# The last norm of a two-layer step: three tiles by ScalarE and GpSimd, two by VectorE

## The reference, cut to what matters

```
x = x + gate2 * hierarchical_moe(h2, ...)
...
def rms_norm(x, g):
    xf = x.astype(jnp.float32)
    y = xf * lax.rsqrt(jnp.mean(xf * xf, axis=-1, keepdims=True) + EPS)
    return (y * g.astype(jnp.float32)).astype(x.dtype)

y_prompt = rms_norm(xp, final_norm)
y_sample = rms_norm(xs, final_norm)
```

## Time and profile before

| | us |
|---|---|
| median of 3 runs | 1088.19 |
| lowest and highest of them | 1087.49, 1089.31 |
| the profiled execution: its time | 1088.57 |
| the profiled execution: its span | 1086.6 |

### The profile page before, as it was taken

One profiled execution on the slowest core, in us unless ns is written; L12 is line 12 of the kernel. 1 busy time (PEld: TensorE's weight loads), 2 busy tenths in 40 slices (PEclk: granted clock), 3 DMA queues, 4 the chain that ended last, 5 costly groups with the idle time before them and its releaser, 6 DMA issues.

```text
span 1086.6 us, 16043 instructions
## 1 busy us (share of the span) xinstructions
PE 993.7 (91%) x5720; PEld 765.0 (70%) x5720; DVE 672.6 (62%) x966; ACT 585.9 (54%) x929; POOL 250.6 (23%) x304
## 2 busy tenths in 40 slices
PE   5999989997998799999989999899779969999994
PEld 2688865765776588877847888467668758888771
DVE  0359125655256799889653941465635679998956
ACT  4452235655233488888366321465633348898822
POOL 3033016211041122231310410620112321222031
PEclk9999998998899899999999999899999989999997
DMA  9785226643155999999780240556423269999954
GB/s 317 268 274 199 78 63 252 225 157 117 59 209 196 345 388 411 404 403 359 257 267 19 83 150 10 198 184 228 154 97 136 85 231 344 411 420 407 370 188 173
DMA packets 89091, 248.17 MB, mean 228 GB/s; under 512 B 25772, under 2 KB 30380, under 8 KB 79816
## 3 DMA queue, kind: packets, MB, share of 16 engines
q1 hardware_dynamic: 75960, 209.54, 51.9%
q0 software_dynamic: 11632, 32.60, 8.5%
q10 hardware_dynamic: 1440, 5.24, 1.2%
HBM read 220.82 MB, written 30.21 MB: 231 GB/s over the span
## 4 chain that ended last, share of the span: by engine, by line
PE 66%; DMA 11%; DVE 9%; ACT 7%; issue 4%; SPq 1%; POOL 0%; ACTq 0%; POOLq 0%; DVEq 0%
PE ps L1592 11%; PE ps L1594 11%; PE ps L1593 11%; DMA pool<-in_moe_w 6%; PE ps L1610 4%; DMA raw<-in_moe_w 3%; PE ps L1788 3%; PE ps L1803 3%; PE ps L1599 3%; PE ps L1601 3%; PE ps L1600 3%; DVE wL L1378 2%; PE ps L1777 2%; ACT wH L960 2%; PE ps L2027 2%
## 5 line engine op out<-in xcount | busy, mean ns | idle before, releaser
L1592 PE MATMUL ps<-wH,actH 128*128 128x512 f32 x600 | 243.0, 405 | 6.1 <-DVE actL L1127 2.5
L1594 PE MATMUL ps<-wH,actL 128*128 128x512 f32 x600 | 235.8, 393 | 0.0
L1593 PE MATMUL ps<-wL,actH 128*128 128x512 f32 x600 | 235.0, 392 | 0.0
L1378 DVE TENSOR_TENSOR wL<-raw,wH 128x2048 fp32r<-128x2048 f32 x64 | 146.3, 2287 | 13.0 <-ACT wH L960 12.7
L1592 PEld LDWEIGHTS ps<-wH,actH 128*128 128x128 f32 x600 | 113.7, 189 | 33.9 <-issue 6.2
L960 ACT ACTIVATE wH<-raw 128x2048 fp32r<-128x2048 f32 x64 | 122.3, 1913 | 25.6 <-DMA raw<-in_moe_w 25.6
L1594 PEld LDWEIGHTS ps<-wH,actL 128*128 128x128 f32 x600 | 113.3, 189 | 25.1
L1593 PEld LDWEIGHTS ps<-wL,actH 128*128 128x128 f32 x600 | 113.8, 190 | 21.5
L1599 PE MATMUL ps<-wH,actH 128*128 128x512 f32 x256 | 104.1, 407 | 6.1 <-DVE actL L1499 3.4
L1601 PE MATMUL ps<-wH,actL 128*128 128x512 f32 x256 | 100.8, 394 | 0.0
L1600 PE MATMUL ps<-wL,actH 128*128 128x512 f32 x256 | 99.8, 390 | 0.0
(11 more groups left out here) (270 smaller groups left out, 1715.3 us busy)
## 6 DMA issues: line engine op xcount, KB each, us to landing
raw<-in_moe_w SPq DMA_DIRECT2D x96, 512.0 KB, 8.3
raw<-in_w_ada SPq DMA_DIRECT2D x40, 1024.0 KB, 5.0
raw<-in_moe_w SPq DMA_DIRECT2D x16, 1024.0 KB, 13.9
pool<-in_moe_w SPq DMA_DIRECT2D x32, 512.0 KB, 7.9
pool<-in_moe_w SPq DMA_DIRECT2D x16, 1024.0 KB, 13.1
ys<-pool SPq DMA_DIRECT2D x32, 512.0 KB, 12.9
raw<-in_w_in SPq DMA_DIRECT2D x15, 1024.0 KB, 8.9
raw<-in_w_ada SPq DMA_DIRECT2D x16, 512.0 KB, 12.2
```

Of the source, the lines that this page charges most:

```text
L1378: dve.tensor_tensor(wL[:, w, :], mraw[parity][i], f32(wH[:, w, :]), ALU.subtract).then_inc(sem(f"m_lo{i}"), 1)
L1592: pe.matmul(out, aH, wH[:, slot_, cols_], start=first, stop=False)
L1593: pe.matmul(out, aH, wL[:, slot_, cols_], start=False, stop=False)
L1594: return pe.matmul(out, aL, wH[:, slot_, cols_], start=False, stop=last)
```

## The change

For tiles 0, 1 and 2 the final norm leaves VectorE. ScalarE does the product with the factor per token (`norm1_scale` into `xr[t]`, the form that layers 0 and 1 begin with), and GpSimd then multiplies by `frow` (`final_row`, a new function) and writes `x[:, t, :]`. Tiles 3 and 4 stay with `final_norm` on VectorE; ahead of the first of these VectorE waits until the three products of GpSimd are done, so that `y_final` counts the tiles in order. GpSimd's product for tile t-1 stands behind its `rstd` pair of tile t, and ScalarE's scaling of tile t-1 behind its squaring of tile t.

```
+TAIL = 3
...
-                rstd1(l + 1)
+                if l + 1 < DEPTH:
+                    rstd1(l + 1)
+            l = DEPTH
+
+            def final_row(t):
+                pl.wait_ge(sem("xr_ready"), at("xr_ready", l, t + 1))
+                pl.tensor_tensor(x[:, t, :], xr[t], frow, ALU.mult).then_inc(sem("y_final"), 1)
+
+            pl.wait_ge(sem("final_row"), 16)
+            for t in range(NT):
+                rstd(stat[:, t:t + 1], stat[:, 8 + t:9 + t], 1, D, sem("ss1"), at("ss1", l, t + 1), sem("rstd1"))
+                if 1 <= t <= TAIL:
+                    final_row(t - 1)
...
             def norm1_scale(l, t):
 
-                if l < DEPTH:
+                if l < DEPTH or t < TAIL:
...
             def final_norm(t):
+                if t == TAIL:
+                    dve.wait_ge(sem("y_final"), TAIL)
...
-                    if l == DEPTH - 1 and t:
+                    if l == DEPTH - 1 and t > TAIL:
                         final_norm(t - 1)
```

## The result

The changed kernel takes 1091.01 us (median of 7 runs, 1089.11 to 1095.08), the kernel before on the same chip 1087.93 (7 runs, 1085.23 to 1090.86). The ratio is 1.0030, with a 95% interval of 1.0016 to 1.0044: slower by some 3.3 us, between 1.7 and 4.8. The interval holds the forecast of +3.2 and also the +4.4 of the prediction's first rival; the trace tells them apart, not the time.

A forecast was written before the change was run, and what follows sets the result against it. GpSimd's last rstd pair, with its 9.5 us drain, was taken to bound the kernel; products and adds holding each other delay it from 1076.92 to 1080.11, +3.2 on the median 1088.19: 1091.4 us, range 1089.6 to 1093.4.

The forecast's parts named there:

- the prediction's first rival: At tile 2, GpSimd's first product wins over VectorE's add and TensorE ends late: +4.4, 1092.6 us; chance 0.28.
- first product, held: GpSimd's product for tile 0 asks 0.09 behind the add of tile 2, is held, and ends at 1069.73.
- end of the last pair: GpSimd's rstd pair of tile 4, behind the third product: ends at 1080.11, 3.2 us later than before.
- The bound: At the kernel's end, GpSimd's last rstd pair sets the time, with its 9.5 us closing drain behind it.
- The rival of the untied drain: GpSimd's closing drain isn't tied to its last instruction and still ends at 1086.4: +-0, 1088.2 us; chance 0.09.
- The price of a product: Each of GpSimd's new 128x1024 products costs 2.36 us, with bounds of 2.32 and 2.56.
- The exclusion: VectorE's two-SBUF-input and GpSimd's SBUF-reading instructions exclude each other: end 3.2 us later with it, 0.4 earlier without.
- One order inside the tail: First half of tile 4's pair beside the norm of tile 3, second half held by it until 1080.11.
- The sign of an add of tile 4 over 2 us long: Expected in the new trace: VectorE's add of tile 4 (L1587), held by GpSimd's second product, over 2 us long.
- The rival without exclusion: GpSimd's products and VectorE's adds run side by side, adds at TensorE's pace: -0.4, 1087.8 us; chance 0.08.
- The rival of the first product: GpSimd's first product goes ahead of tile 2's add, delaying TensorE's tile 4: +4.4, 1092.6 us; chance 0.28.

The follow-up runs named there:

- the pairs taken away: Kernel before, factors per token of tiles 3 and 4 (or tile 4 alone) made by ScalarE and VectorE, not GpSimd: 0.9955 (tile 4 alone: 0.9970) against before.
- the run with memsets: Changed kernel with each of GpSimd's three products replaced by a memset of the same length that reads no SBUF: 0.9989 against the kernel before.
- The run with the late add: Changed kernel with a 256-column memset on VectorE ahead of tile 2's product, so tile 2's add comes after GpSimd's first product begins: 1.0047 against before.
- the run through PSUM: Changed kernel with VectorE's gate-row product written back to PSUM in the last tail, so the add has one SBUF input: 1.0021 against the kernel before.

## Why the prediction was right

Each time below counts from TensorE's last matmul (1071.90 in the prediction's sum, 1069.15 in the trace after); the predicted ones are those of the sum.

| step | predicted | measured |
|---|---|---|
| first product, held | 3.36 long | 3.29 |
| second and third product | 2.36 long | 2.35, 2.34 |
| end of the add of tile 4 | 3.27 | 3.17 |
| end of the last pair | 8.21 | 8.16 |
| end of the last norm | 9.59 | 9.55 |
| end of the span | 17.9 | 17.9 |

- **The bound** (GpSimd's last pair, with the drain behind it) held, and was open when the prediction was made: one drain in one trace couldn't show what it hangs on. The extra memset on GpSimd, the extra norms on VectorE and the pairs taken away show it from three sides. The rival of the untied drain falls.
- **The price of a product**, from the line through 512 and 1280 columns, was right to 0.02 us. The estimate of 2.25 from the Trainium skill ("GPSIMD Engine Reference", Performance versus the Vector engine) was 0.1 too low, and the trace's rows decided rightly.
- **The exclusion** was the term that carried the sum, and its offset of 0.14 (the held instruction needs its own length less that) fits: the add of tile 4 ends at 1072.32, which is the product's end at 1071.24 + 1.23 - 0.15. The rule of the Trainium skill ("SBUF — State Buffer", Who interferes with whom) agrees with the traces, also in that a GpSimd instruction which only writes doesn't conflict with VectorE's two inputs (memsets of 2.40 beside adds of 1.22). That the holder keeps the other out for its whole length stands there of VectorE's two-port modes; for two-input instructions the product of 3.29 and the add of 3.20 show it here.
- **One order inside the tail was wrong.** The prediction let the first half of the last pair in ahead of the norm of tile 3, and had its second half held. In the trace the norm goes first (1075.35, against 1075.39), the first half takes 1.28 and the second is free (0.55, where about 1 was named as a sign). From the end of the third product to the end of the pair it is 2.00 and not 1.82. That the total came out at 8.16 against 8.21 is luck by these 0.2 us: the third product had ended 0.23 earlier than summed (6.16 against 6.39). The sign of an add of tile 4 over 2 us long wasn't met either: it took 1.87, and the prediction's own sum gave 1.98.
- **The rival without exclusion falls**, since the add of tile 4 took 1.87 and not 1.23 beside a product. Its price of -0.4 was for a chip in which nothing is held, and no run is that case: with memsets and through PSUM the last pair ends 0.7 to 0.8 above before, because the norm of tile 3 still holds half of it. Without these 1.1 us the run with memsets would have ended its pair at 5.77 - 1.09 = 4.68, which is 0.3 under the 5.02 of before, so the price fits. What a reader can take from the two runs is that even with the adds free the tail ends 0.7 to 0.8 later than before.
- **The rival of the first product** was not what the trace shows, by a margin of 0.16 (1063.58 against 1063.74; predicted 0.09). The run with the late add shows that it costs 1.4 more, where 1.2 was worked out. The order can turn by itself: in the trace of the run through PSUM TensorE waited 0.78 for a gather ahead of tile 2, and the product came first (1064.93 against 1064.99). Whether some of the seven runs of the changed kernel fell into it isn't known: their times spread by 6 us, those of before by 5.6, and only one has a trace.

## What to carry to other kernels

Before work is moved from VectorE to GpSimd, look at what both do at that moment: a two-input elementwise instruction on each, all in SBUF, is not parallel work but a queue of two, and a chain that goes from one to the other pays in both directions. In these traces an input in PSUM took VectorE out of the conflict. Then look past the last computing instruction at each queue's closing drain: in this kernel GpSimd's took 9.5 us in all nine traces, so two pairs of 0.8 us taken from GpSimd's end gave 5.5 us of tail, while 2.5 us more on VectorE cost at most 0.2. Whether a kernel without gathers on GpSimd has the same drain wasn't tried.

## What the runs showed of the hardware that was not expected

- GpSimd's closing drain lasts 9.5 us from the end of its last instruction: 10.08 from its start in seven of the eight traces with the pair last (10.09 in the other), and 13.09 with a memset of 3.08 behind the pair. ScalarE's and VectorE's end with their last instruction (in the kernel before at 1076.0 and 1078.4, with the last instructions ending at 1076.0 and 1078.3). What the 9.5 us are spent on no run shows.
- VectorE writing a product back to PSUM and adding from there costs nothing: both instructions keep 1.22 to 1.23 us for 128x1024.
- A delay of 0.3 us turns an order and moves the end by 1.4: with the add of tile 2 first the product is held for 0.9, with the product first the add is held for 2.0 and TensorE stands for 1.6.
- The square and the square root on ScalarE needed one table load between them (1.28 us, ahead of the first tile), and the root with the reciprocal took 0.29 and 0.16, so ScalarE and VectorE made the factor per token no slower than GpSimd: the last norm starts 4.9 us behind TensorE's end (1077.02 - 1072.16), and 5.1 in the kernel before (1077.02 - 1071.90).
